# A product of two by two blocks with seven block products in the last expert stage of a 1-core kernel

## What is computed

```python
act = jax.nn.gelu(jnp.einsum("chkd,cd->chk", u_sel, xc))
v_sel = jnp.take(v, idx, axis=0)
return jnp.einsum("chk,chkd->cd", act * gates, v_sel)
```

## Time and profile before

| | us |
|---|---|
| median of 3 runs | 1356.86 (1356.63 to 1357.43) |
| the profiled execution | 1356.07 |
| its span, first to last instruction | 1354.2 |
| TensorE busy | 1328.5 (98%) |
| VectorE busy | 950.0 (70%) |
| ScalarE busy | 769.3 (57%) |
| GpSimd busy | 442.6 (33%) |
| mean granted TensorE clock | 0.995 |

### The profile page before, as it was taken

How to read it: one execution, slowest core, us unless ns; L and a number is a source line. 1 busy time by engine, 2 the same in 40 slices (tenths; PEclk the granted TensorE clock), 3 DMA queues, 4 the chain that set the end, 5 groups by cost and what they waited for, 6 DMA issues and landing times.

```text
span 1354.2 us, 26679 instructions
## 1 busy us (share of the span) xinstructions
PE 1328.5 (98%) x9169; PEld 1209.0 (89%) x9169; DVE 950.0 (70%) x1751; ACT 769.3 (57%) x1379; POOL 442.6 (33%) x254
## 2 busy tenths in 40 slices
PE   7999999999998999999999999999999999999997
PEld 7998979988978988999999999999988888888886
DVE  4687567656676974899989888889545555555555
ACT  6545454444556355477767676676545555555554
POOL 1100424000115661079887666666720000000000
PEclk9999999999999999999999999999999999999999
DMA  8533136555553444445554444444455555555553
GB/s 298 170 109 110 32 131 189 189 193 191 188 171 128 154 142 142 165 167 179 189 185 155 157 147 154 154 154 145 166 188 189 186 186 186 187 187 190 187 189 129
DMA packets 62177, 225.29 MB, mean 166 GB/s; under 512 B 7168, under 2 KB 7680, under 8 KB 61712
## 3 DMA queue, kind: packets, MB, share of 16 engines
q1 hardware_dynamic: 60512, 218.36, 48.1%
q10 hardware_dynamic: 1584, 5.84, 1.2%
HBM read 223.12 MB, written 1.05 MB: 166 GB/s over the span
## 4 chain that ended last, share of the span: by engine, by line
PE 95%; DVE 2%; ACT 1%; issue 1%; DMA 0%; POOL 0%; POOLq 0%; DVEq 0%; ACTq 0%
PE bank L532 83%; PE bank L1071 3%; PE bank L633 1%; PE bank L779 1%; PE bank L765 1%; PE bank L589 1%; PE bank L1026 1%; DVE arena L2081 0%; PE bank L934 0%; PE bank L564 0%; DMA h<-in_x 0%; PE bank L949 0%; PE bank L514 0%; PE bank L594 0%; PE bank L770 0%
## 5 line engine op out<-in xcount | busy, mean ns | idle before, releaser
L1164 ACT ACTIVATE w_hi<-ring 128x1024 fp32r<-128x1024 f32 x414 | 439.5, 1062 | 512.4 <-PE bank L532 327.0
L1715 DVE TENSOR_TENSOR w_lo<-ring,w_hi 128x1024 fp32r<-128x1024 f32 x259 | 317.2, 1225 | 272.9 <-ACT w_hi L1164 272.4
L532 PE MATMUL bank<-hT_hi,w_hi 128*128 128x256 f32 (+2 forms) x1696 | 420.6, 286 | 0.0
L532 PE MATMUL bank<-hT_lo,w_hi 128*128 128x256 f32 (+2 forms) x1696 | 412.9, 282 | 0.0
L1667 POOL TENSOR_TENSOR w_lo<-ring,w_hi 128x1024 fp32r<-128x1024 f32 x128 | 310.4, 2427 | 158.2 <-ACT w_hi L1164 157.9
L532 PEld LDWEIGHTS bank<-hT_lo,w_hi 128*128 128x128 f32 x1696 | 320.4, 189 | 0.4
L532 PEld LDWEIGHTS bank<-hT_hi,w_hi 128*128 128x128 f32 x1696 | 318.9, 188 | 0.4
L532 PE MATMUL bank<-hT_hi,w_lo 128*128 128x256 f32 (+2 forms) x1696 | 234.7, 280 | 0.0
L532 PEld LDWEIGHTS bank<-hT_hi,w_lo 128*128 128x128 f32 x1696 | 216.0, 189 | 0.0
L532 PE MATMUL bank<-w_hi,wgt_lo 128*128 128x512 f32 x504 | 199.6, 396 | 0.0
L532 PE MATMUL bank<-w_hi,wgt_hi 128*128 128x512 f32 x504 | 199.3, 395 | 0.0
(11 more groups left out here) (360 smaller groups left out, 1681.4 us busy)
## 6 DMA issues: line engine op xcount, KB each, us to landing
ring<-in_stream SPq DMA_DIRECT2D x414, 512.0 KB, 3.5
arena<-in_rows ACTq DMA_DIRECT2D x1, 1536.0 KB, 10.7
consts<-in_consts ACTq DMA_DIRECT2D x1, 1152.0 KB, 5.6
arena<-in_keys ACTq DMA_DIRECT2D x1, 1024.0 KB, 6.2
h<-in_x SPq DMA_DIRECT2D x1, 512.0 KB, 5.1
h<-in_x ACTq DMA_DIRECT2D x1, 512.0 KB, 5.3
arena<-in_rows ACTq DMA_DIRECT2D x1, 512.0 KB, 3.7
out_h<-arena SPq DMA_DIRECT2D x2, 256.0 KB, 2.1
```

Source lines behind the costliest of these rows:

```text
L532: mm = nc.tensor.matmul(o, a, b, start=first and not low_part and xp is x[0], stop=last and low_part)
L1164: nc.scalar.activation(w_hi[:, g % S, :], ring[:, g % R, :], ACT.Copy).then_inc(hi_done, 1)
L1715: nc.vector.tensor_tensor(w_lo[:, g % S, :], ring[:, g % R, :], w_hi[:, g % S, :].bitcast(F32), ALU.subtract).then_inc(lo_done, 1)
```

## The change

Two tiles n, n + 1 give a product of two by two blocks: tokens by halves of 128, features by halves of 512, and the experts of the two tiles as the inner dimension. Written out it has eight block products of 128 x 128 x 512. The change computes it in Winograd's form with seven block products: with sums of the blocks of V (T1, T3 from one VectorE operation, T2, T4 on GpSimd) and of the row blocks (X3, S1, X2, X4 on VectorE). The products go to banks 0, 1, 2 directly and to banks 4 to 7, which hold terms that belong to several outputs. These are added to h with signs, by eight VectorE additions, once, behind the last pair (`h_add`).

- The 128 tiles are 32 bodies of four. The first `FAST` = 5 bodies and the last body stay as they were. In the 26 (`PAIRS`) between, the first two tiles are a pair (21 matmuls, `pair_products`) and the other two are plain tiles (24 matmuls).
- Every operand of a pair is split too. For each pair ScalarE makes high parts of W11 (`w11_copy`), of T1 and T3 (`t13_copy`), of W21 and W22 (`w2_copy`), of the four row sums (`x_copy`), of T2 and T4 (`t24_copy`). VectorE makes the sums T1 and T3 (`first_sums`), the row sums and the low parts of W11, W21 and W22 (`row_sums`), and the low part of the row sums (`x_low`). GpSimd makes T2 = T1 + W22, T4 = T2 + W21 and the low parts of all four T (`low_sums`). These stand in each engine's loop between the work for the plain tiles.
- All sums and parts lie in SBUF: sums T in `consts`, row sums in `idxT`, high and low parts in the arena, `hT_hi` and `hT_lo`, places that are free by then. There is one set of buffers, so GpSimd's sums and low parts of a pair release the first sums of the next (`pair_more_lo`), and TensorE's use of the products releases the copies (`pair_used`).
- SyncE loads the first tile of the next pair after the low part of W11, the second after the low part of W21 and W22 and after T4.
- `open_sums` is gone; the first tile opens banks 0 to 3, the first pair banks 4 to 7.

The core of the diff, first TensorE's part:

```diff
-            open_sums()
-            with pe.Fori(0, N_KEYS // PEER_BODY - 1) as i:
-                for j in range(PEER_BODY):
...
+                a11 = wgt_hi[:, 0, 0:P], wgt_lo[:, 0, 0:P]
+                a12, a22 = ((wgt_hi[:, 1, t * P:(t + 1) * P], wgt_lo[:, 1, t * P:(t + 1) * P]) for t in range(NT))
+                x3, s1, x2, x4 = ((pair_x_hi[:, n, :], pair_x_lo[:, n, :]) for n in range(4))
+                pe.wait_ge(wgt_out, n0 + 1)
+                pe.wait_ge(pair_hi, pair_hi0 + 1 + 5 * k)
+                step(4, a11, pair_w_hi[:, W11, :])
+                pe.wait_ge(pair_lo, pair_lo0 + 1 + 3 * k)
+                low_step(4, a11, pair_w_lo[:, W11, :]).then_inc(pair_used, 1)
+                pe.wait_ge(pair_hi, pair_hi0 + 4 + 5 * k)
+                pe.wait_ge(pair_lo, pair_lo0 + 3 + 3 * k)
+                step(5, s1, pair_t_hi[:, T1, :])
+                step(7, x3, pair_t_hi[:, T3, :])
+                pe.wait_ge(pair_more_lo, pair_more_lo0 + 1 + 2 * k)
+                low_step(5, s1, pair_t_lo[:, T1, :])
+                low_step(7, x3, pair_t_lo[:, T3, :]).then_inc(pair_used, 1)
...
+                step(0, a12, pair_w_hi[:, W21, :])
+                step(1, x4, pair_w_hi[:, W22, :])
...
+                step(6, x2, pair_t_hi[:, T2, :])
+                step(2, a22, pair_t_hi[:, T4, :])
```

ScalarE's loop, one round for each body with a pair behind it:

```diff
+            with act.Fori(0, PAIRS - 1) as k:
+                n0 = k * 4 + 4 * FAST
+                first_rows(k, n0)
+                w11_copy(k + 1)
+                t13_copy(k + 1)
+                w2_copy(k + 1)
+                third_rows(k, n0)
+                x_copy(k + 1)
+                t24_copy(k + 1)
+                act.wait_ge(tiles_done, tiles_counted(4 * FAST + 2) + 2 * k)
+                copy_rows(n0 + 4, 0, 1)
+                tile_hi(tiles_counted(4 * FAST + 6) + 2 * k, 2, ring_round(2, FAST + 1) + k)
```

GpSimd's whole part:

```diff
+            def low_sums(k, first):
+
+                pool.wait_ge(pair_hi, pair_hi0 + (5 if first else 2) + 5 * k)
+                both = slice(first, first + 2)
+                nc.gpsimd.tensor_tensor(pair_t_lo[:, both, :], pair_t[:, both, :], pair_t_hi[:, both, :].bitcast(F32),
+                                        ALU.subtract).then_inc(pair_more_lo, 1)
+
+            with pool.Fori(0, PAIRS) as k:
+                pool.wait_ge(pair_sums, pair_sums0 + 1 + 4 * k)
+                pool.wait_ge(pair_more_lo, pair_more_lo0 + 2 * k)
+                nc.gpsimd.tensor_tensor(pair_t[:, T2, :], pair_t[:, T1, :], pair_ring[:, B22, :], ALU.add)\
+                    .then_inc(pair_more, 1)
+                pool.wait_ge(pair_more, pair_more0 + 1 + 2 * k)
+                nc.gpsimd.tensor_tensor(pair_t[:, T4, :], pair_t[:, T2, :], pair_ring[:, B21, :], ALU.add)\
+                    .then_inc(pair_more, 1)
+                low_sums(k, T1)
+                low_sums(k, T2)
```

VectorE's, with the order at the entry and in the loop:

```diff
+            def first_sums(k):
+
+                for j in range(2):
+                    dve.wait_ge(slot_full[(G_V + j) % R], 16 * (RING_V + FAST + k))
+                dve.wait_ge(pair_more_lo, pair_more_lo0 + 2 * k)
+                nc.vector.tensor_tensor(pair_t[:, T1:T3 + 1, :], pair_ring[:, B11:B22 + 1:3, :],
+                                        over(pair_ring[:, B12, :], 2), ALU.add).then_inc(pair_sums, 1)
...
+            def row_sums(k, blocks):
+
+                nc.vector.tensor_tensor(pair_x[:, X3:S1 + 1, :], over(blocks[:, 1, :], 2), blocks[:, 0:4:3, :],
+                                        ALU.subtract).then_inc(pair_sums, 1)
+                pair_low(k, 1, pair_w_lo[:, W11, :], pair_ring[:, B11, :], pair_w_hi[:, W11, :])
...
+                pair_low(k, 3, pair_w_lo[:, W21:W22 + 1, :], pair_ring[:, B21:B22 + 1, :], pair_w_hi[:, W21:W22 + 1, :])
...
+            tile_lo(tiles_counted(n + 2), 2)
+            rows_low(n + 2, 2)
+            first_sums(0)
+            row_sums(0, act_blocks[:, 2 * n + 8:2 * n + 12, :])
+            tile_lo(tiles_counted(n + 3), 3)
+            rows_low(n + 3, 3)
+            x_low(0)
+            rows_low(n + 4, 0, 1)
+            tile_lo(tiles_counted(n + 6), 2)
+
+            with dve.Fori(0, PAIRS - 1) as k:
+                n0 = k * 4 + 4 * FAST
+                rows_low(n0 + 1, 1)
+                first_sums(k + 1)
+                tile_lo(tiles_counted(4 * FAST + 3) + 2 * k, 3)
+                rows_low(n0 + 2, 2)
+                row_sums(k + 1, act_blocks[:, bass.ds(k * 8 + 8 * (FAST + 1), 4), :])
+                rows_low(n0 + 3, 3)
+                x_low(k + 1)
+                rows_low(n0 + 4, 0, 1)
+                tile_lo(tiles_counted(4 * FAST + 6) + 2 * k, 2)
...
+            h_add(part, part, bank[4][:, :], ALU.subtract)
+            h_add(h_part(0), h_part(0), bank[4][:, :], ALU.add)
+            h_add(h_part(2), h_part(2), part, ALU.subtract, 1)
+            h_add(part, part, bank[5][:, :], ALU.add, 3)
+            tile_lo(tiles_counted(N_KEYS - 4), 0)
```

More of the change, by code:

```diff
@@ L60, with tiles_counted @@
 G_V = G_PEER + N_KEYS
+FAST = 5
+BODIES = N_KEYS // PEER_BODY
+PAIRS = BODIES - 1 - FAST
+RING_V = G_V // R + 1
+def tiles_counted(n):
+    if n < 4 * FAST:
+        return G_V + n + 1
+    if n >= 4 * (BODIES - 1):
+        return G_V + 4 * FAST + 2 * PAIRS + n - 4 * (BODIES - 1) + 1
+    return G_V + 4 * FAST + 2 * (n // 4 - FAST) + n % 4 - 1
 ROUTED = 44
@@ new lines, in fast_body @@
+            def fast_body(k, n0, first=False, last=False):
+                pair_products(k, n0, first, last)
+                for j in (2, 3):
+                    plain_tile(tiles_counted(4 * FAST + j) + 2 * k, n0 + j, j)
+            pe.sem_inc(pair_used, 4)
+            for n in range(4):
+                plain_tile(tiles_counted(n), n, n, n == 0)
+            with pe.Fori(0, FAST - 1) as i:
+                for j in range(4):
+                    plain_tile(i * 4 + tiles_counted(4 + j), i * 4 + (4 + j), j)
@@ L1104, in _ @@
+            fast_body(0, 4 * FAST, True)
+            with pe.Fori(1, PAIRS - 1) as k:
+                fast_body(k, k * 4 + 4 * FAST)
+            fast_body(PAIRS - 1, N_KEYS - 8, last=True)
+            for n in range(N_KEYS - 4, N_KEYS - 2):
+                plain_tile(tiles_counted(n), n, n)
+            closing_rows([(tiles_counted(n) - 1, [wgt_lhs(n, t) for t in range(NT)], (wgt_out, n + 1))
                           for n in (N_KEYS - 2, N_KEYS - 1)], 0, 3)
@@ L2340, in _, with tile_lo @@
                     wgt_low(j, row(act_all, i * PEER_BODY + (j + 2)), i * PEER_BODY + (j + 2))
-            for n in range(N_KEYS - PEER_BODY, N_KEYS - 2):
-                lo(G_V + n + S)
+            def tile_lo(count, j):
+                dve.wait_ge(hi_done, count)
+                dve.wait_ge(tiles_done, count - S)
+                nc.vector.tensor_tensor(w_lo[:, j % S, :], ring[:, (G_V + j) % R, :], w_hi[:, j % S, :].bitcast(F32),
+                                        ALU.subtract).then_inc(lo_done, 1)
```

192 lines of the change are left out of this document (174 added, 18 removed).

## The result

The changed kernel takes 1493.16 us (median of 4 runs, 1484.38 to 1495.52), the kernel before 1356.74 (4 runs, 1354.78 to 1357.43). The ratio is 1.0995, with a 95% interval of 1.0971 to 1.1019: slower, as forecast, but 53 us above the predicted 1440.3 and 13 us above the upper end of the range.

What follows compares the result with a forecast made beforehand. TensorE bounds the kernel before; in pair bodies VectorE and GpSimd exclude each other. Bodies +77.5, last pair's body -0.7, entry +7.3, end +0.2, zeros -0.9 sum to +83.4 us: 1440.3 us, upper end 1480, lower bound 1428 less 3 us.

Steps and rivals of the forecast that it cites:

- the port: Pair bodies: VectorE operations with two SBUF inputs and GpSimd's SBUF reads exclude each other, 14.3 us a body, +77.5 us.
- the rival in which nothing is excluded: Pair bodies: VectorE and GpSimd overlap, holding times come to 10.5 us or less, TensorE stays the bound, 1342.9 us; chance 0.08.
- The body without the clock: A pair body at full TensorE clock: 14.3 us, against 11.2 before and 10.5 of TensorE's own work.
- The sum of the holds: Holding times in one pair body: VectorE 7.0 us plus GpSimd 7.26 us, together 14.3 us.
- Whole durations: Pair body by the Trainium skill's rule, blocking for whole instructions: 8.8 + 7.3 = 16.1 us, 128 us slower than before.
- The clock: TensorE in pair bodies: idling lowers its clock, 1.7 us of work lost, 10.5 becomes 12.2 us, held covered by 14.3.
- The entry: Ahead of the first pair: TensorE stalls 4.9 us for tile 19, 2.4 more for T2 and T4, together 7.3 us.
- The end: Last pair's body without GpSimd work, -0.7 us; eight additions into h ahead of tiles 124 to 126's low parts, +0.2 us.
- The loads: Rival at the pairs' loads: landings of over 6 us would make bodies 15 us and more, 1460 us; chance 0.18 shared.
- The signs: Expected in the pair stage's timeline: 14.3 us bodies, GpSimd's 1024 over 2.43 us, VectorE's well over 1.225, some 147 GB/s.
- the second rival: Pair stage: exclusion plus lowered TensorE clock, 1461 us with half the effect, 1483 with all; chance 0.18 shared with late loads.
- Its other upper bound: Pair bodies at 15.5 us, from hand-overs costing 0.1 to 0.2 us more each: 1472 us.

Runs made afterwards that it cites:

- run 1: Changed kernel with GpSimd's four operations of a pair cut to 16 columns of each block, all waits kept: 1344.19 us, ratio 0.9919.
- run 3: Changed kernel with GpSimd's four operations on 16 columns and a memset filling the rest, so it writes but hardly reads: 1344.48 us, ratio 0.9914.
- run 4: Changed kernel with one input of each of VectorE's 13 operations read from PSUM bank 3, GpSimd's work whole: 1344.41 us, ratio 0.991.
- run 2: Changed kernel with 13 products of zeros added ahead of the body's second plain tile, filling TensorE's wait: 1452.04 us, ratio 1.0713.
- run 7: Changed kernel with GpSimd's four operations of a pair on half of their columns: 1391.56 us, ratio 1.0261, body 12.36 us.
- run 8: Changed kernel with GpSimd's four operations of a pair on three quarters of their columns: 1424.9 us, ratio 1.0507, body 13.64 us.
- run 6: Changed kernel with 27 plain bodies ahead and only 4 pairs in place of 26 (FAST = 27): 1378.59 us, ratio 1.0171.
- run 10: Changed kernel with GpSimd's operations cut to 16 columns and a 3.88 us VectorE reduction ahead of the last tile's row-block low part: 1448.83 us, ratio 1.068.
- run 5: Changed kernel with GpSimd's four operations moved to VectorE, nothing left out: 1369.3 us, ratio 1.0101, body 11.45 us.

## Why the prediction went as it did

**The direction, and its reason: right.** The chance for slower was 0.91, most of it for the port. Runs 1, 3 and 4 show the exclusion and its condition as it was read from the earlier trace rows: with GpSimd's reads gone, or VectorE's second input in PSUM, the body is 10.44 to 10.48 us and the kernel takes 1344 us, close to the 1342.9 of the rival in which nothing is excluded. The rival was sized well; its condition did not hold.

**The body without the clock: 14.3 forecast, 14.59 measured (run 2).** The sum of the holds came out well partly by luck. VectorE's list is 7.64 us from start to start (4 x 1.13 + 2 x 0.60 + 4 x 0.33 + 3 x 0.20), not 7.0. GpSimd blocks it for 0.987 x 14.59 - 7.64 = 6.8 us, not for 7.26, though the sums of 512 take 1.30 us and not 1.22. Runs 7 and 8 show that the sum of holds is not the law of this loop: at half, VectorE is busy for 0.907 x 12.36 = 11.2 us (7.64 + 3.6 blocked) and idle for 1.1, at three quarters 12.8 and 0.8. At full size and full clock VectorE is busy for 98.7%, and of the three sizes this is the only one where the two ways of counting meet. Whole durations, 16.1 us in the prediction, lie nearer to the 16.34 measured, but that is luck too: 1.75 us of the 16.34 are the clock's.

**The clock: the step that failed.** The prediction had the mechanism as a rival and priced it at 1461 with half and at 1483 with all of it, but set it aside with "The port's 14.3 still covers it". It does not. The slow tile is not beside the port's work but in line with it: tile 3 follows the wait, the copy of the next row block follows tile 3, and VectorE's list follows the copy. So what tile 3 loses comes on top of the port's time. I had compared a sum for TensorE (12.2) with a sum for the port (14.3) and taken the larger. That holds for engines that run freely beside each other, not for ones that wait in turn.

What it loses: twelve matmuls at 0.427 in place of 0.233 us are 2.3 us at most. In the fifteen bodies with the whole tile at the lower level the body is 16.7 us against 14.5 in run 2, so 2.2 us of this come through. The missing part is time in which VectorE would have been late anyway: in run 2 it starts the next row block 0.4 us after ScalarE's copy is done, and 0.2 us after it in the changed kernel. In the other ten bodies only a part of the tile is slow and 1.1 to 1.3 us come through. The mean over both is the 1.75 us between run 2 and the changed kernel. That this is so near to the 1.7 us of the prediction, taken from one place, is luck: a whole slow tile costs more, and ten bodies have none that is wholly slow.

Of the 53 us that were missing 1.75 x 25 = 44 us are the clock's, 0.29 x 25 = 7 us the body without it, and 4 us the entry; this adds up to 2 us too much.

**The entry: 7.3 forecast, 11 measured.** TensorE wanted tile 19 at 1040.08 and got it at 1048.77, and the tile itself then ran slowly, to 1054.01. VectorE's, GpSimd's and TensorE's lines that show it:

```profile
1041.65 2.31 DVE L2617 TENSOR_TENSOR idxT<-arena,idxT 128x128 f32<-128x128 f32 x1
...
1046.15 2.56 DVE L2592 TENSOR_TENSOR wgt_lo<-arena,wgt_hi 128x256 fp32r<-128x256 f32 x1
```

```profile
1041.43 2.39 POOL L1903 TENSOR_TENSOR hT_lo<-consts,hT_hi 128x1024 fp32r<-128x1024 f32 x1
1045.65 2.78 POOL L1903 TENSOR_TENSOR hT_lo<-consts,hT_hi 128x1024 fp32r<-128x1024 f32 x1 [1.84 <-ACT hT_hi L1676]
```

```profile
1048.77 0.79 PE L606 MATMUL bank<-w_hi,wgt_hi 128*128 128x512 f32 x1 [8.52 <-DVE wgt_lo L2592]
```

I had let T2 and T4 come between. Both of GpSimd's low parts came as well. The first stood beside X4, which took 2.31 us in place of 0.29, the second beside the low part of tile 19's row block, the last operation ahead of this tile, which took 2.56 us in place of 0.42. So the stall is 8.5 us, and the slow tile adds 5.24 - 2.80 = 2.4 us. Run 6 gives some 11 us by another way.

**The end: near.** The prediction had -0.7 + 0.2 = -0.5 us for the last pair's body and the end, the trace -0.1. From 1440 us on TensorE waits only for the 3.3 us of two ordinary bodies, and behind the first product of the last pair it never waits, so the eight additions into h cost it no wait.

**The loads: right that they are not the bound.** The stage moves 127 to 131 GB/s and VectorE waits for no load in the changed kernel; run 1 moves 199 GB/s with TensorE never waiting.

**The signs.** GpSimd's operations of 1024 have a mean of 2.52 us, over 2.43, as forecast. VectorE's of 1024 were to be well over 1.225 us and are not, 1.22: the smaller ones, of 128 to 512 elements, carry the time. The granted clock of 0.83 was the sign of the second rival.

**The range.** It ended at 1480, with the clock's full price counted as 1483, so one of its own rivals lay outside. Its other upper bound has a slip: 15.5 us a body is 1.2 x 25 = 30 us above 1440, so 1470 and not 1472. With the entry at 11 and the port at 14.6 us, the same full price, 44 us, would have given 1356.07 + 25 x 3.4 + 11 - 1.6 + 44 + 0.8 = 1495. The port's 14.6 lay inside its bounds; I had varied the port, the clock and the entry one at a time and never together.

**What stays open.** Why the same wait costs a whole tile, a part of one or nothing: ten bodies of run 10 and the first of run 6 keep the clock, and ten of the changed kernel lose it for a part of tile 3. The circle of waits is read from timelines and agrees with them; no run tests it by itself. Whether a sparser arrangement, a pair in every second body with all sums on VectorE, would beat the kernel before was not tried; run 5 is 0.25 us a body short of it with a pair in each. No run that computes everything beats the kernel before.

## What to carry to other kernels

Before an idle GpSimd is given work beside VectorE, look at what both read: if VectorE's operations have two SBUF inputs and GpSimd's read SBUF, add their times on one line, as a first estimate (in run 7 it came out 1.7 us a body too low), and compare with VectorE doing it alone, which here was 124 us faster. Where the sum says that TensorE will wait, ask in the same step what it does to its clock, and follow the chain from the slowed work to the next wait: what lies in the circle is added, only what lies beside it is covered. Saved matmuls are worth their 0.233 us only as long as what feeds them has room: the seven products were worth 11 to 12 us in runs 1, 3 and 4, and their preparation cost 149.
